# A chain of transformer layers on one core: five rows of scale factors by transfers in place of matmuls, a narrow projection laid side by side, and steps of the engines' orders moved

## The reference, cut to what matters

```python
def rms_norm(x, g):                                   # scale factors: one number for each token
    y = x * lax.rsqrt(jnp.mean(x * x, axis=-1, keepdims=True) + 1e-6)
    return y * g
# mLSTM: ig and fg are the last 2 * C_HEADS = 16 columns of the projection u = hn @ o_w_in
ig = u[..., o0:o0 + C_HEADS]; o0 += C_HEADS
fg = u[..., o0:o0 + C_HEADS]
# SSD: cb * decay in each of 16 heads, then the heads' outputs times silu(z), and a norm over each of 2 groups
y_diag = einsum('bgecls,bcsgep->bclgep', cb[:, :, None] * decay_in, xc)
y = rms_norm((y * silu(z)).reshape(bsz, seq, SSD_GROUPS, -1), norm_g)
```

## Time and profile before

| | |
|---|---|
| median of 3 runs | 3456.34 us |
| profiled execution, its own time | 3456.34 us |
| its span (first to last instruction) | 3454.4 us |
| PE busy | 3432.0 us, 99% |
| PEld busy | 2931.0 us, 85% |
| DVE busy | 2121.1 us, 61% |
| ACT busy | 1713.8 us, 50% |
| POOL busy | 31.6 us, 1% |
| granted TensorE clock | 9 of 9 tenths in all 40 slices, mean 1.0 |

### The profile page before, as it was taken

The page is one execution under the profiler, slowest core; times in us unless marked ns, Lnnn a source line. Parts: engine busy times, 40 slices in busy tenths (PEclk is TensorE's granted clock), DMA queues, the critical chain, the costliest instruction groups (busy, mean ns, idle before and its releaser), DMA issues.

```text
span 3454.4 us, 43150 instructions
## 1 busy us (share of the span) xinstructions
PE 3432.0 (99%) x18080; PEld 2931.0 (85%) x18080; DVE 2121.1 (61%) x2225; ACT 1713.8 (50%) x2009; POOL 31.6 (1%) x55
## 2 busy tenths in 40 slices
PE   8999999999999999999999999999999999999999
PEld 7888888888888888888888888888888888888887
DVE  8766668454656877655545555577766555455454
ACT  5743464356555475664434434445756644344343
POOL 1000000000000000000000000000000000000000
PEclk9999999999999999999999999999999999999999
DMA  7553655554555544545555555555444455555554
GB/s 245 182 194 134 222 183 174 193 181 172 196 189 180 189 171 147 183 158 184 192 191 189 189 191 193 185 182 192 160 158 171 168 186 195 189 189 192 188 193 158
DMA packets 90241, 633.00 MB, mean 183 GB/s; under 512 B 10416, under 2 KB 10688, under 8 KB 15552
## 3 DMA queue, kind: packets, MB, share of 16 engines
q1 hardware_dynamic: 85392, 610.19, 50.6%
q0 software_dynamic: 4656, 20.06, 1.6%
HBM read 628.07 MB, written 2.13 MB: 182 GB/s over the span
## 4 chain that ended last, share of the span: by engine, by line
PE 93%; DVE 4%; ACT 2%; issue 0%; DMA 0%; SPq 0%; DVEq 0%; ACTq 0%
PE G L580 29%; PE G L582 15%; PE G L572 14%; PE G L573 13%; PE G L574 13%; DVE w_lo L478 2%; ACT w_hi L466 1%; PE M L924 1%; PE G L621 1%; PE G L619 1%; PE G L620 1%; PE M L1252 1%; DVE arena L863 1%; PE G L564 0%; PE G L565 0%; PE G L566 0%
## 5 line engine op out<-in xcount | busy, mean ns | idle before, releaser
L478 DVE TENSOR_TENSOR w_lo<-w_raw,w_hi 128x2048 fp32r<-128x2048 f32 x584 | 1325.7, 2271 | 1112.1 <-ACT w_hi L466 1111.3
L466 ACT ACTIVATE w_hi<-w_raw 128x2048 fp32r<-128x2048 f32 x584 | 1108.6, 1899 | 1418.6 <-PE G L574 721.4
L580 PE MATMUL G<-x_halves,w_hi 128*128 128x512 f32 x4256 | 1343.1, 397 | 9.9 <-DVE w_lo L2718 9.7
L582 PEld LDWEIGHTS G<-x_halves,w_lo 128*128 128x128 f32 x4256 | 799.4, 188 | 187.9
L582 PE MATMUL G<-x_halves,w_lo 128*128 128x256 f32 x4256 | 840.0, 278 | 0.0
L580 PEld LDWEIGHTS G<-x_halves,w_hi 128*128 128x128 f32 x4256 | 649.9, 189 | 13.7 <-DVE w_lo L2718 9.7
L572 PE MATMUL G<-w_hi,y_halves 128*128 128x512 f32 x1640 | 645.5, 394 | 0.9 <-DVE y_halves L1227 0.9
L574 PE MATMUL G<-w_hi,y_halves 128*128 128x512 f32 x1640 | 638.8, 390 | 0.0
L573 PE MATMUL G<-w_lo,y_halves 128*128 128x512 f32 x1640 | 638.4, 389 | 0.0
L572 PEld LDWEIGHTS G<-w_hi,y_halves 128*128 128x128 f32 x1640 | 307.9, 188 | 65.0 <-DVE y_halves L1227 2.5
L574 PEld LDWEIGHTS G<-w_hi,y_halves 128*128 128x128 f32 x1640 | 307.8, 188 | 64.7
(11 more groups left out here) (467 smaller groups left out, 2529.2 us busy)
## 6 DMA issues: line engine op xcount, KB each, us to landing
w_raw<-in_s_up SPq DMA_DIRECT2D x176, 1024.0 KB, 4.8
w_raw<-in_s_down SPq DMA_DIRECT2D x88, 1024.0 KB, 4.8
w_raw<-in_s_ssd SPq DMA_DIRECT2D x40, 1024.0 KB, 4.8
w_raw<-in_s_hgrn SPq DMA_DIRECT2D x32, 1024.0 KB, 4.8
w_raw<-in_s_gate SPq DMA_DIRECT2D x32, 1024.0 KB, 4.8
w_raw<-in_s_mlstm SPq DMA_DIRECT2D x32, 1024.0 KB, 4.8
w_raw<-in_s_mlstm_gate SPq DMA_DIRECT2D x32, 1024.0 KB, 4.8
w_raw<-in_s_o_out SPq DMA_DIRECT2D x16, 1024.0 KB, 4.8
```

The lines of the kernel that those rows point to most:

```text
L466: act.activation(whi[p % SETS][:, 0:n_], raw[p % RAW][:, 0:n_], ACT.Copy).then_inc(S("hi_ready"), 1)
L478: dve.tensor_tensor(wlo[p % RAW][:, 0:n_], raw[p % RAW][:, 0:n_], whi[p % SETS][:, 0:n_].bitcast(F32), ALU.subtract).then_inc(S("lo_ready" ...
L580: pe.matmul(o, hi[:, k, f], x2, start=first, stop=False, skip_group_check=True)
L582: mm = pe.matmul(o[:, 0:T], lo[:, k, f], x2[:, 0:T], start=False, stop=last, skip_group_check=True)
```

## The change

- The five rows: diagonals, products with ones and copies go. POOL stores the 128 x 2 scale factors to a DRAM tensor of 2 x 128 (256 elements of 4 bytes), waits, and loads it into `rrow` in all 128 partitions. `row_dve` becomes a wait for that load, at the same place in DVE's order (`row_moved`).
- The narrow chunk: high and low parts of the 16 columns stand side by side in `w_hi`, 32 columns for each row block, and one matmul of 512 moving columns does both; the low rows are added after the transpose.
- Orders: HGRN's first eight steps on DVE at p - 0.25; `masked(0)` and `masked(1)` on DVE from 18 to 17.75; `lora_half` entered behind the pair steps of the same piece on ACT and DVE; `square_sums` 0 and 1 on PE from 29 and 31 to 29.125 and 31.125; cross attention: on PE `values(2)` from 11.25 to 11 and `values(3)` from 11.5 to 11.25, on ACT and DVE turn 3 and values 2 and 3 from 11 and 11.5 to 10.75.

```diff
+        plans["mlstm"][8].tall = 32
+            pair = whi[p % SETS][:, 0:512].rearrange("p (k n) -> p k n", n=32)
+            return pair[:, :, 0:16], pair[:, :, 16:32], raw[p % RAW][:, 0:256].rearrange("p (k n) -> p k n", n=16)
+            if p == side_by_side:
+                hi, _, both_ = side_tiles(p)
+                act.activation(hi, both_, ACT.Copy).then_inc(S("hi_ready"), 1)
...
+                hi, lo, both_ = side_tiles(p)
+                dve.tensor_tensor(lo, both_, hi.bitcast(F32), ALU.subtract).then_inc(S("lo_ready"), 1)
...
+                                mm = pe.matmul(base[0:32, 0, :], whi[p % SETS][:, 32 * k:32 * k + 32], x2, start=first,
+                                               stop=last, skip_group_check=True)
...
-            for t in range(NT):
-                mm = pe.matmul(M[:, (g - 1) % 4, t * P:t * P + P], one[:, 0:1].to_broadcast([P, P]), diag[:, t, :],
-                               start=True, stop=True, skip_group_check=True)
         def row_dve(dve):
-            g = n(dve, "ring")
-            dve.wait_ge(S("fm_full"), g)
-            dve.tensor_copy(rrow[:], M[:, (g - 1) % 4, 0:T]).then_inc(S("fm_lo"), 1)
-            dve.wait_ge(S("fm_lo"), g)
+            dve.wait_ge(S("row_moved"), n(dve, "row_moved", 32))
...
-            for t in range(NT):
-                ins = dve.tensor_scalar(diag[:, t, :], ident[:, :], norm_rstd(e)[:, t:t + 1], None, ALU.mult)
-            ins.then_inc(S("diag_ready"), 1)
...
+                    link(dve, dve.tensor_copy(o, src[:, :, c0:c0 + w]))
+                    ins = dve.tensor_tensor(o, o, src[:, :, low:low + w], ALU.add)
...
-                layer_at(pe, l, 29 + 2 * j if j < 3 else 34.5, lambda j=j: square_sums(j))
+                layer_at(pe, l, 29.125 + 2 * j if j < 2 else (33, 34.5)[j - 2], lambda j=j: square_sums(j))
...
-            at(11, lambda: turn(3))
-            at(11.25, lambda: values(2))
-            at(11.5, lambda: values(3))
+            at(11, lambda: turn(3), lambda: values(2))
+            at(11.25, lambda: values(3))
...
-            at(11, lambda: att_turn_act(act, 3, xa["pt"], False, l))
-            at(11.5, lambda: att_values_act(act, 2, 0, l), lambda: att_values_act(act, 3, 0, l))
+            at(10.75, lambda: att_turn_act(act, 3, xa["pt"], False, l), lambda: att_values_act(act, 2, 0, l),
+               lambda: att_values_act(act, 3, 0, l))
...
+            layer_at(dve, l, 17.75, lambda: masked(0))
+            layer_at(dve, l, 17.75, lambda: masked(1))
             layer_at(dve, l, 18, start)
             for k in range(8):
                 layer_at(dve, l, 19 + k, lambda k=k: pair(k))
+            for j in range(4):
+                layer_at(dve, l, 15 + 2 * j, lambda j=j: lora_half(j))
...
+            def spread_rstd(j, e):
+                pool.wait_ge(S("rstd_ready"), NORMS.index(e) + 1)
+                pool.dma_start(dram[f"row_{e}"].rearrange("t p -> p t"), norm_rstd(e), allow_slow_non_contiguous=True
+                               ).then_inc(S("row_moved"), 16)
+                pool.wait_ge(S("row_moved"), 32 * j + 16)
+                load(rrow[:], dram[f"row_{e}"].rearrange("t p -> (t p)").partition_broadcast(P), "row_moved")
...
+            for j, p in enumerate(HGRN_STEPS):
+                at_piece(dve, first_piece["hgrn"] + (p - 0.25 if j < 8 else p), lambda: next(program, None))
```

More of the change, by code:

```diff
@@ L1033, in turns_pe, with tail_pe, tail_act @@
             return {q * (j + 1) + (q > 1): [first if j == 0 else lambda j=j: turn_pe(pe, name, j)] for j in range(3)}
[L1035 to L1043, removed]
+        def tail_pe(pe, name, at):
+            return {at: [lambda: turn_pe(pe, name, 3)]}
+        def tail_act(act, dst, gain, e, at):
             feed = {at: [lambda: act_fm(act, KT, dst, 0, gain, pairs=range(6, 8))]}
@@ L1084, in rows_turn_dve @@
             src = M[:, (g - 1) % 4, 0:T].rearrange("p (t f) -> p t f", f=P)
-            for o, c0, w in parts:
-                ins = dve.tensor_copy(o, src[:, :, c0:c0 + w])
+            for o, c0, w, low in parts:
+                if low is None:
+                    ins = dve.tensor_copy(o, src[:, :, c0:c0 + w])
+                else:
+                    link(dve, dve.tensor_copy(o, src[:, :, c0:c0 + w]))
+                    ins = dve.tensor_tensor(o, o, src[:, :, low:low + w], ALU.add)
             ins.then_inc(S("fm_lo"), 1)
@@ L1744, in ssd_act @@
             layer_at(act, l, 14, softplus)
-            for j in range(4):
-                layer_at(act, l, 15 + 2 * j, lambda j=j: lora_half(j))
             layer_at(act, l, 16, scores)
@@ L1749, in ssd_act @@
                 layer_at(act, l, 18 + k, lambda k=k: exps(k))
+            for j in range(4):
+                layer_at(act, l, 15 + 2 * j, lambda j=j: lora_half(j))
             layer_at(act, l, 24, lora_roots)
@@ L2246, in ssd_dve @@
             layer_at(dve, l, 14, times_dt)
-            for j in range(4):
-                layer_at(dve, l, 15 + 2 * j, lambda j=j: lora_half(j))
             layer_at(dve, l, 16, scan)
             layer_at(dve, l, 17, columns_in)
+            layer_at(dve, l, 17.75, lambda: masked(0))
+            layer_at(dve, l, 17.75, lambda: masked(1))
             layer_at(dve, l, 18, start)
@@ L2459, in _ @@
             load(ple_in[:], dram["pT"][1].rearrange("(k p) t -> p k t", p=P), "p_loaded")
+            spread_rstd(0, "mlstm")
             pool.wait_ge(S("piece_done"), started("o_out", 3))
@@ L2486, in _ @@
                     load(mem_parts[j], dram["memT"][:, 8 * j:8 * j + 8, :], "mem_loaded")
+                spread_rstd(2 * l + 2, f"ffn{l}")
             for j, c in enumerate(plans["down12"][0:3]):
@@ L2623, in _ @@
             act_gemm(act, "gate0", feed)
[L2624 removed]
+            feed = tail_act(act, halves["y"], "o_norm", "mlstm", -0.5)
             feed[18] = [lambda: n(act, "fm_full")]
@@ L2652, in _ @@
                 else:
-                    feed = tail_act(act, halves["x"], "attn1", "attn1", 1, -0.5)
+                    feed = tail_act(act, halves["x"], "attn1", "attn1", -0.5)
                 ssd_act(act, l)
@@ L2783, in attn0_scales @@
                 rstd_dve(dve, "attn0", "final")
-                diag_dve(dve, "attn0")
             for l in range(2):
@@ L2899 @@
         dram[name] = nc.dram_tensor(f"in_{name}", a.shape, mybir.dt.from_np(a.dtype), kind="ExternalInput").ap()
+    for e in ("mlstm", "attn0", "ffn0", "attn1", "ffn1"):
+        dram[f"row_{e}"] = nc.dram_tensor(f"row_{e}", (NT, P), F32).ap()
     for l in range(2):
```

66 lines of the change are left out of this document (29 added, 37 removed).

## The result

The changed kernel takes 3487.6 us (median of 5 runs, 3485.7 to 3490.4) against 3456.3 of the kernel before: 1.0092 times the time, 95% interval 1.0079 to 1.0104. It is slower by 31 us; forecast was 3444.6. The profiled execution is the slowest of the five: 3490.4 us, span 3488.6, 34.2 longer than before.

What follows compares the result with a forecast made beforehand. PE, busy 3432.0 of 3454.4 us, was taken as the bound. Rows 1.5, narrow chunk 1.9, HGRN 1.4, pairs 5.5, squares 1.6, cross attention -0.2 make 11.7 us off 3456.34: 3444.6 us, range 3441.0 to 3453.0.

Steps and rivals of the forecast that it cites:

- What comes: Five rows: store and load chain takes 11 us at mlstm, 7 to 8 elsewhere, upper end 12; PE stalls 1.0 at mlstm.
- Rival E: Five rows: the store of 256 separate elements takes long; past 12 us each microsecond costs 5; 15 us gives 3467; chance 0.06.
- The prediction's own sign of being wrong: DVE standing more than 3 us at `row_dve` in attn0, or PE's waits behind the pairs keeping more than 2 us.
- The leads: Splits behind `row_dve`: an 11 us chain stalls PE 1.0 at mlstm; 12 us loses 4.5 at attn0, 0.5 at attn1.
- The row work that goes: PE's work and waits at the five rows: 1.1 at mlstm, 0.9 at attn0, 0.45 at the others; 3.35 us in all.
- Narrow chunk: Its 16 row blocks lose the second matmul each, 0.12 us apart: 1.9 us off PE.
- HGRN: DVE's steps moved ahead of a split: PE's waits at two levels go, gain 1.4 us, ends 0.9 and 1.4.
- Pairs: PE's waits for pairs of SSD heads go, with masks earlier and `lora_half` behind: 5.5 us gained, ends 3 and 5.8.
- squares: Sums of squares one row block later on PE; four of six move: 1.6 us gained, ends 0.7 and 1.7.
- Cross attention: Wait for head 2's low half goes, 0.65 twice; new wait at `values(2)` about 0.75, twice: net 0.2 us lost.
- Rival D: Reordered steps only move PE's waits; only rows and narrow chunk remain, 3.4 us gained, 3452.9; chance 0.12.
- B: Rows land two weight pieces late, 12 us at all five; they lose 6.0 in place of gaining 1.5: 3452.1; chance 0.15.

Runs made afterwards that it cites:

- the kernel with one load: Changed kernel without the stores; POOL loads 256 numbers of a gain vector into the row, not the right factors: 3442.59 us, ratio 0.9961.
- three loads: Changed kernel with three 1 KB loads in a chain in place of store and load, not the right factors: 3460.56 us, ratio 1.0014.
- blocks: Changed kernel, but DVE first turns the factors, stored by two transfers of 4 elements of 128 bytes: 3447.59 us, ratio 0.9975.
- 8 bytes: Changed kernel with factors stored as 128 elements of 8 bytes, the row read with a stride of two: 3451.18 us, ratio 0.9986.
- with the stores: Changed kernel with rows made the old way, plus the five 4-byte-element stores, read by nobody: 3446.20 us; the same without stores 3446.51.

## Why the prediction was wrong

**The step that failed** is "What comes", where the chain was bounded: at most 12 us from the factors to the row, "each transfer lands only with the weight piece that is on its way". By that count, which starts 0.3 to 0.6 us ahead of the store's issue, it was 16.4 to 20.3. The store had been bounded by the 2.2 us of `acs` and a weight piece's 4.8, and `acs` is 16 long elements; alone, such a store takes 1.7 and the change's 8.1. Rival E named this and what it costs, "Past 12 us every further microsecond stops PE at all five places", but had 0.06, on the ground that 512 KB take 4.8 us. Bytes were the wrong measure. So was the page's 2 us of fixed cost: the Trainium skill, "DMA: Bandwidth & Descriptors", "Anatomy of one DMA", has the time go by fixed cost and bytes, which roughly holds here for long elements (1.5 to 1.7 us) and fails by a factor of four for neighbouring 4-byte ones. The read-modify-write below 512 B, in its table of specifications, pointed the right way, yet 4-byte elements 64 bytes apart took 2.0, and no run here shows the mechanism. The prediction's own sign of being wrong came: DVE stood 10.0 us at the row in attn0, where it allowed 3.

**E's own sum** gives, for the mean chain of 17.8 us, 3452.1 + 5 x 5.8 = 3481.1; the profiled execution took 3490.4. The 9.3 us that are left are about what the clock cost, which the prediction didn't consider. Against the kernel with one load (span 3440.7, PE busy 3424.3) the changed kernel's span is 47.9 us longer. PE's idle time for DVE at the norms is 35.8 of that, and 10.6 are in its busy time (3434.9 for as many matmuls), the matmuls at half clock behind each stall. With three loads PE is busy 3426.9, with one half-clock stretch in place of five: 2.6. The Trainium skill, "TensorE: Matmul & The Clock Gate", section "Part 1: The HAM clock gate", has PE fall to 1.2 GHz behind idle time, and the rows agree: a stall of this length is paid a second time, here by 1.6 us at mlstm (3.1 us of matmuls at half clock).

**The leads** behind `row_dve` were read well; what was wrong is only the length of the chain that they were held against. By the prediction's count a stall of 1.0 for 11 us was said at mlstm, and a microsecond more for each further one: 11.2 left PE idle for 1.1 (blocks), 12.7 for 2.6 (8 bytes), and the change's 17.6 for 7.5. At attn0, "12 us: 4.5 lost"; 12.2 lost 5.9 (8 bytes), of which 5.1 idle. At attn1 12 us were to lose 0.5 net of 0.45 of row work, so PE would wait 0.95, and it waited 1.0 (blocks); at the two ffn 0.5 by the same sum, and 0.3 and 0.4 (blocks).

**The row work that goes** was 3.35 us: the pieces are 1.1, 0.9 and three times 0.45 shorter, as said. With a short chain it stays, except for 0.35 of attn0's, and the times go from 3446.5 to 3442.6; of these 3.9 us the pieces named explain 3.0, and the rest is spread in amounts too small to place. L1381's wait, said to grow to about 1, is 0.6.

**Narrow chunk** 1.9, measured 1.9. **HGRN** 1.4, measured 1.4. **Pairs** 5.5 and **squares** 1.6, together 7.1, measured 6.8; the sums' wait is down to two places as said. **Cross attention**: the wait at L1210 came, 0.5 us twice in place of 0.7 (the earlier trace rows bounds it), the old one went, and the stage is as long as before; -0.2 was said. In all 10.2 was said without the rows and 9.7 was measured. Rival D falls.

**The idle time** was not all within reach. Of the 22 us in which PE stood, 9.7 are the wait for the first split, and one line of the list of waits before is in no sum of the prediction:
```profile
PE G L1201 <- DVE ple_in L1178: 1.0, 2, 0.5
```
Both are there after the change too (9.6 and 1.0).

Of the change's parts only the rows came out with the wrong sign. The range was wrong too: its upper end, 3453.0, took in B and D and left E out because no row showed such a store, and that was the reason to widen it.

## What to carry to other kernels

A transfer's price is not in its bytes: before an order is built on one whose element size and layout no trace shows, time it alone, and take single 4-byte elements written side by side to DRAM for about five times a store of long rows (8.1 us for 1.5 to 1.7 here). What waits for a transfer in an engine's fixed order has a lead that can be read from the profile (here 6 to 11 us); within it the transfer is free, and beyond it each microsecond is paid at every place, and again in the granted clock, as at every stall of 5.3 us and more here. A change that mixes good and bad parts is worth taking apart: of this one, 10 us of gain lay under 41 of loss.

## What the runs showed of the hardware that I had not expected

- 256 elements of 4 bytes written from 128 partitions to adjacent places in DRAM took 7.7 to 8.4 us with nothing beside them, and 8.5 to 13.0 beside the weights; 64 bytes apart they took 2.0 to 2.6 alone. 128 elements of 8 bytes took 3.0 to 3.6, 128 of 16 bytes 1.7. Read back in the same pattern: 2.4 to 2.5. Why neighbours are slow stays open.
- Such a store holds other traffic up (130 GB/s in place of 198 over 9 us), and five pieces of weights in buffers hid that wholly (3446.2 us with the stores, 3446.5 without).
- A row of 1 KB loaded into 128 partitions takes 4.2 to 4.5 us alone and 3.2 to 8.0 beside the weights.
- PE's granted clock fell to half in or just behind each stall of 5.3 us and more, one of 3.7 and one of 2.6, and not at one of 2.75, one of 2.2 and the shorter ones. In the changed kernel it was at half for 6.8 us at four norms and 10.2 at the last, part of it while PE still stood.
- A DVE product whose second operand is read with a stride of two float32 takes as long as one without (692 ns).
